# A two-block model on one core: the scratch fill is moved in a queue, columns are waited for by pairs, norms are done by token halves

## The reference, cut to what matters

```python
h = x
for layer in range(2):                       # first block
    if layer == 0:
        h = h + even_mixer(rmsnorm(h))       # short convolution and window means, w_in, w_out
    else:                                    # GLU, 31-tap depthwise convolution, layer norm over channels
        h = h + conformer_conv(rmsnorm(h))
    h = h + cross_attn(rmsnorm(h), mem)      # 4 heads of 256; k, v = split(rmsnorm(mem) @ wkv)
    if layer == 0:
        h = h + swiglu(rmsnorm(h))           # width 2816
    else:
        h = h + moe_swiglu(rmsnorm(h))       # 8 experts of width 3584, the two best per token
x = rmsnorm(h)
h = layer_norm(x)                            # second block
y = hybrid_mixer(h)                          # "fox" attention with forget gates, differential attention, HGRN recurrence
h = layer_norm(ALPHA * h + y)
y = memory_attention(h, mem_2)               # the third attention over a memory
h = layer_norm(ALPHA * h + y)
y = grouped_moe(h)                           # 16 experts of width 512 in 4 groups, two of one group per token
out = layer_norm(ALPHA * h + y)
```

## Time and profile before

| | us |
|---|---|
| median of 3 runs | 2263.54 |
| lowest and highest | 2256.84, 2264.5 |
| profiled execution | 2261.9 |
| its span in the profile | 2260.1 |

### The profile page before, as it was taken

The page is one execution under the profiler, slowest core; times in us unless marked ns, Lnnn a source line. Parts: engine busy times, 40 slices in busy tenths (PEclk is TensorE's granted clock), DMA queues, the critical chain, the costliest instruction groups (busy, mean ns, idle before and its releaser), DMA issues. The chain is left out here.

```text
span 2260.1 us, 30543 instructions
## 1 busy us (share of the span) xinstructions
PE 2184.1 (97%) x11738; PEld 1874.1 (83%) x11738; DVE 1727.9 (76%) x1606; ACT 1362.8 (60%) x1202; POOL 83.3 (4%) x79
## 2 busy tenths in 40 slices
PE   7999999999989999999999999999999999899997
PEld 7888999967877888888888888888779888788886
DVE  4655555697658888888888988888856664698897
ACT  4454433417437777777777777777646344477775
POOL 2000000000001000000000000000000000000000
PEclk9999999999999999999999999999989999999998
DMA  9442565532269999999999999999744161699995
GB/s 303 171 170 93 184 203 190 189 112 75 84 223 354 377 377 381 373 384 376 388 363 392 367 385 368 391 362 396 290 148 160 74 218 44 242 370 380 377 379 214
DMA packets 274825, 617.26 MB, mean 273 GB/s; under 512 B 9537, under 2 KB 34321, under 8 KB 274737
## 3 DMA queue, kind: packets, MB, share of 16 engines
q1 hardware_dynamic: 265648, 584.43, 70.7%
q0 software_dynamic: 9088, 31.60, 4.5%
HBM read 603.41 MB, written 12.58 MB: 273 GB/s over the span
## 5 line engine op out<-in xcount | busy, mean ns | idle before, releaser
L2424 DVE TENSOR_TENSOR w_low<-ring,w_high 128x2048 fp32r<-128x2048 f32 x426 | 971.2, 2290 | 142.3 <-ACT w_high L1705 141.8
L1705 ACT ACTIVATE w_high<-ring 128x2048 fp32r<-128x2048 f32 x426 | 815.1, 1917 | 166.0 <-PE ps L791 166.0
L790 PE MATMUL ps<-w_high,parts 128*128 128x512 f32 (+2 forms) x1896 | 736.5, 388 | 0.0
L789 PE MATMUL ps<-w_high,parts 128*128 128x512 f32 x1560 | 617.9, 396 | 12.6 <-DVE w_low L2424 7.8
L791 PE MATMUL ps<-w_low,parts 128*128 128x512 f32 x1560 | 609.1, 390 | 0.0
L790 PEld LDWEIGHTS ps<-w_high,parts 128*128 128x128 f32 x1896 | 357.6, 189 | 69.3
L789 PEld LDWEIGHTS ps<-w_high,parts 128*128 128x128 f32 x1560 | 293.5, 188 | 74.7 <-DVE w_low L2424 11.6
L1894 DVE TENSOR_TENSOR w_low<-ring,w_high 128x2048 fp32r<-128x2048 f32 (+2 forms) x117 | 262.0, 2253 | 110.3 <-ACT w_high L1428 104.3
L791 PEld LDWEIGHTS ps<-w_low,parts 128*128 128x128 f32 x1560 | 293.1, 188 | 62.7
L789 PE MATMUL ps<-XT_high,w_high 128*128 128x256 f32 x1024 | 294.5, 288 | 9.4 <-DVE parts L1885 7.4
L1428 ACT ACTIVATE w_high<-ring 128x2048 fp32r<-128x2048 f32 (+2 forms) x117 | 219.7, 1884 | 135.4 <-PE ps L791 127.0
(11 more groups left out here) (440 smaller groups left out, 1659.8 us busy)
## 6 DMA issues: line engine op xcount, KB each, us to landing
ring<-in_od_moe_gu SPq DMA_DIRECT2D x224, 1024.0 KB, 8.1
ring<-in_od_moe_down SPq DMA_DIRECT2D x112, 1024.0 KB, 7.8
ring<-in_w SPq DMA_DIRECT2D x96, 1024.0 KB, 8.6
ring<-in_ev_ffn_gu SPq DMA_DIRECT2D x22, 1024.0 KB, 7.6
ring<-in_xa_wkv SPq DMA_DIRECT2D x8, 2048.0 KB, 8.6
ring<-in_od_pw_w SPq DMA_DIRECT2D x6, 2048.0 KB, 8.0
ring<-in_w_in SPq DMA_DIRECT2D x6, 2048.0 KB, 8.0
ring<-in_ev_ffn_down SPq DMA_DIRECT2D x11, 1024.0 KB, 5.1
```

Of the source, the lines that this page charges most:

```text
L789: mm(out_, xh, wh, start=start, stop=False)
L790: mm(out_, xl, wh, start=False, stop=False)
L1705: A(w_high[:, j % SPLITS, :], ring[:, j % NS, :], ACT.Copy).then_inc(moe_sem(k, "high"), 1)
L2424: V.tensor_tensor(w_low[:, j % SPLITS, :], ring[:, j % NS, :], w_high[:, j % SPLITS, :].bitcast(F32), SUB)\
```

## The change

- GpSimd: the two fills of `sums[1]` wait for H and stand ahead of `row(0, ln_in_g_2)`; the fill for k = 2 stays where it was.
- TensorE: `project` of plain units, when first, waits for columns pair by pair. The wait for all columns goes from "B" and from `route(2)`, which now waits pair by pair too.
- TensorE: in "A" the wait for `in_gc` and 20 `keep_busy` transposes ahead of Ak0; `keep_busy` 75 becomes 80 and 90 becomes 50.
- ScalarE: the first six diagonals are written ahead of the copy of Bv1; the first half of fqk is rounded ahead of the squares; a root of a constant loads its table ahead of the norm after the third attention.
- VectorE: the additions Co0 and Co1 are made by halves with accumulated sums, and the norm after them adds those instead of reducing H. Every norm of the second block but the last signals `h_ready` after each half, and fqk and `route(2)` turn H by halves (`turn_by_tokens`).

```diff
...
+            def fill_sums(k, dst):
+                pool.dma_start(sums[k][T:T + P, :], dst[:, 0, :]).then_inc(moe_sem(k, "rows_added"), 16)
+                pool.dma_start(sums[k][0:T, :].rearrange("(a p) d -> p a d", p=P), dst[:, :, :]).then_inc(S("rows_stored"), 16)
+
             def expert_rows(k, source, ready, value, dst):
...
                     pool.wait_ge(S("xs_ready"), 7)
+                    fill_sums(k, dst)
                 else:
-                    pool.wait_ge(S("h_updated"), 4)
-                pool.dma_start(sums[k][T:T + P, :], dst[:, 0, :]).then_inc(moe_sem(k, "rows_added"), 16)
-                pool.dma_start(sums[k][0:T, :].rearrange("(a p) d -> p a d", p=P), dst[:, :, :]).then_inc(S("rows_stored"), 16)
-                if k == 1:
                     pool.wait_ge(S(ready), value)
...
             row(0, ins["od_norm_moe"][0].partition_broadcast(P))
+            pool.wait_ge(S("h_updated"), 4)
+            fill_sums(1, H)
             row(0, ins["ln_in_g_2"].partition_broadcast(P))
...
                 row(0, ins["ln_b_2"][0, j].partition_broadcast(P))
-            expert_rows(2, H, "h_ready", 3, XS)
+            expert_rows(2, H, "h_ready", 6, XS)
...
                         for kc in range(KC):
+                            if first and fb == 0 and kc % 2 == 0:
+                                made = "act" if kc < 4 else "vector"
+                                pe.wait_ge(S("columns_by_" + made), seen[made] - 2 + kc % 4 // 2 + 1)
                             last = mm(pair[:, fb // 2, fb % 2 * T:fb % 2 * T + T], w[:, kc, fb * P:(fb + 1) * P],
...
+            def turn_by_tokens(src, ready, n):
+
+                pe.wait_ge(S("columns_by_act"), seen["act"])
+                pe.wait_ge(S("columns_by_vector"), seen["vector"])
+                seen["act"] += 4
+                seen["vector"] += 4
+                for tc in range(HALVES):
+                    pe.wait_ge(S(ready), n - 1 + tc)
+                    for kc in range(KC):
+                        o = kc % 2 * T + tc * P
+                        last = nc.tensor.transpose(ps[:, 4 + kc // 2, o:o + P], src[:, tc, kc * P:(kc + 1) * P], IDENT)
+                        if tc == 1 and kc % 2:
+                            last.then_inc(S("turned"), 1)
+
             def columns_ready():
...
                 turn(XS, ready, value, parts=(tag != "B"))
-                if tag == "B":
-                    columns_ready()
+                if tag == "A":
+                    evicted("in_gc")
+                    keep_busy(20, 2 * (UNIT["Ak0"] % 2))
                 for name in ("k0", "k1", "v0", "v1"):
...
                 if k == 2:
-                    turn(src, ready, value)
-                    columns_ready()
+                    turn_by_tokens(src, ready, value)
                 pe.wait_ge(S("router_split"), 1)
...
                             turn_half(1)
-                        column_pair(kc)
+                    column_pair(kc)
                     for part in (XT_high, XT_low):
...
                 if k == 1:
-                    keep_busy(75, 0)
+                    keep_busy(80, 0)
                 pe.wait_ge(S("added"), 4 * k)
...
-            turn(H, "h_ready", 1)
+            turn_by_tokens(H, "h_ready", 2)
             upto, ones = c_("upto"), ONES
...
             project("Cv1", halves=(0,))
-            turn_ahead(H, "h_ready", 2)
+            turn_ahead(H, "h_ready", 4)
             project("Cv1", halves=(1,))
...
-            keep_busy(90, 6)
-            route(2, "h_ready", 3, H)
+            keep_busy(50, 6)
+            route(2, "h_ready", 6, H)
             experts(2, H)
...
-            def memory_projections(tag, gain):
+            def memory_projections(tag, gain, diagonal=None):
                 if tag == "B":
...
                         highs(halves_to("pw2_1", -1))
+                        for i in range(DIAGONALS):
+                            diagonal(i)
                     if tag == "C" and j == 1:
...
                     highs(halves_to("value1"))
-            memory_projections("B", ("xa_norm_mem", 8))
-            for b in range(TAPS_ON_PE):
-                for k in range(CONV):
-                    i = b * CONV + k
-                    if i >= DIAGONALS:
-                        act.wait_ge(S("diagonal_used"), i - DIAGONALS + 1)
-                    A(w_(5376, DIAGONALS, P)[:, i % DIAGONALS, :], IDENT, ACT.Copy,
-                      scale=vec("od_dw_w", KC * k + KC - TAPS_ON_PE + b)).then_inc(S("diagonal_ready"), 1)
+            def diagonal(i):
+                b, k = divmod(i, CONV)
+                if i >= DIAGONALS:
+                    act.wait_ge(S("diagonal_used"), i - DIAGONALS + 1)
+                A(w_(5376, DIAGONALS, P)[:, i % DIAGONALS, :], IDENT, ACT.Copy,
+                  scale=vec("od_dw_w", KC * k + KC - TAPS_ON_PE + b)).then_inc(S("diagonal_ready"), 1)
+
+            memory_projections("B", ("xa_norm_mem", 8), diagonal)
+            for i in range(DIAGONALS, TAPS_ON_PE * CONV):
+                diagonal(i)
             act.wait_ge(S("diagonal_used"), TAPS_ON_PE * CONV)
...
             A(table_root, ONES[:, 0:1], ACT.Sqrt)
+            highs(halves_to("fqk", -1))
             squares(H, "moe_done", 1, XS, False)
-            highs(halves_to("fqk", -1))
             layer_norm(w_(6144, HALVES, D))
...
             attention("C", 2, None, None)
+            A(table_root, ONES[:, 0:1], ACT.Sqrt)
             layer_norm()
...
                     ins = V.tensor_tensor(h, h, PAIRS[u % 2], ADD)
+                elif name in ("Co0", "Co1"):
+                    for tc in range(HALVES):
+                        at = 2 * tc + j
+                        ins = V.scalar_tensor_tensor(h[:, tc, :], h[:, tc, :], scale, PAIRS[u % 2][:, tc, :], MUL, ADD,
+                                                     accum_out=halves_sum[:, at:at + 1])
                 else:
...
-            def layer_norm(signal, src=H, beside=None):
+            def layer_norm(signal, src=H, beside=None, summed=False):
                 n_["ln"] += 1
-                step(V.tensor_reduce(mean, src[:, :, :], X, ADD))
+                if summed:
+                    step(V.tensor_tensor(mean, halves_sum[:, 0::2], halves_sum[:, 1::2], ADD))
+                else:
+                    step(V.tensor_reduce(mean, src[:, :, :], X, ADD))
                 V.tensor_scalar(mean, mean, -1.0 / D, None, MUL).then_inc(S("mean_ready"), 1)
...
                     last = V.scalar_tensor_tensor(H[:, tc, :], centred[:, tc, :], rstd[:, tc:tc + 1], b, MUL, ADD)
+                    if tc == 0:
+                        last.then_inc(S(signal), 1)
                 use_row(1 - gain_row[0], last)
+                dve.sem_inc(S(signal), 1)
                 gain_row[0] = 1
-                dve.sem_inc(S(signal), 1)
...
                 last = V.scalar_tensor_tensor(H[:, tc, :], centred[:, tc, :], rstd[:, tc:tc + 1], w_(11264, D), MUL, ADD)
+                if tc == 0:
+                    last.then_inc(S("h_ready"), 1)
             use_row(1, last)
...
             attention("C", 2, None)
-            layer_norm("h_ready")
+            layer_norm("h_ready", summed=True)
...
```

## The result

The changed kernel takes 2245.43 us (median of four runs, 2245.22 to 2245.94); the kernel before 2260.19 (four runs, 2256.47 to 2264.5, three of them those shown above). The ratio is 0.9934, its 95% interval 0.9911 to 0.9957: faster by 0.66%, a little more than the 0.5% that can be told from no change. Forecast were 2247 us. The profiled execution took 2245.53 us, its span is 2243.7.

The account below looks back on a forecast made before the run. TensorE, busy nearly the whole span, was taken as the bound, through its waits and half clock. Terms 9.2 + 2.4 - 0.8 + 0.9 + 5.0 = 16.7 us off 2261.9 gave 2245.2, plus 1.6 for the median: 2247 us, range 2238 to 2255.

Parts of the forecast that it names:

- fills ahead: First mixture: earlier fills on GpSimd end ScalarE's wait and TensorE's wait for piece 3 with its half clock; 9.2 us.
- transposes ahead of Ak0: Ahead of Ak0: 20 transposes fill TensorE's idle time so the matmuls behind run at full clock; 2.4 us.
- columns by pairs, diagonals: Conformer: TensorE's taps end earlier, but VectorE sets the end and half clock follows the idle time; -0.8 us.
- first fqk half: Norm before fqk: rounding moves into ScalarE's idle time, so the centred squares come earlier; 0.9 us.
- norm after the third attention: Sums with the additions, table load ahead, halves and pairs shorten the way to the second router; 5.0 us.
- clock elsewhere: Half clock outside the places the steps name: no term in the forecast sum.
- rival (d): Half clock longer at the conformer, or at Ak0 despite the transposes; costs 2 to 7 us, 2251 us; 16%.
- New half clock outside the conformer: Sign that the forecast is wrong: half clock newly appearing anywhere but the conformer; no size given.
- Rival (a): Fox scores: the half clock at 1675.7 to 1692.7, costing 5 to 7 us, goes away; 2240 us; 15%.
- (b): First mixture: the fill is not what frees ScalarE, or lands late again; only 7.5 us gained, 2256 us; 7%.
- (c): First mixture: the weight stream becomes the bound if a landing takes over about 15 us; 2280 us; 2%.

Follow-up runs that it names:

- 1: The changed kernel with the two fills of sums[1] put back behind row(0, ln_in_g_2) on GpSimd: 2256.0 us.
- 11: The kernel before with only the two fills of sums[1] moved ahead of the row load in GpSimd's queue: 2250.34 us.
- 5: The changed kernel without the 20 transposes ahead of Ak0: 2247.0 us.
- experiment 2: The changed kernel with the full wait for the second memory's columns and all diagonals written after Bv1 is taken, as before: 2244.91 us.
- 8: The changed kernel with the first rounded half of fqk behind the squares again: 2245.78 us.
- experiment 7: The changed kernel with the additions Co0 and Co1 undivided and without sums, the norm reducing H again: 2250.41 us.
- 6: The changed kernel with 90 instead of 50 busy transposes behind the third attention, ahead of the second router: 2249.97 us.
- experiment 9: The changed kernel with ten transposes added in TensorE's 1.24 us idle time ahead of the fox scores: 2238.67 us.
- experiment 3: The changed kernel with 60 instead of 16 busy transposes ahead of the conformer's sums of squares: 2245.49 us.
- experiment 4: The kernel before, unchanged, run and profiled once more: 2258.82 us over ten runs.
- 12: The changed kernel with four idle times filled by transposes, plus transposes ahead of the first router, each scatter and at the last level: 2234.51 us.

## Why the prediction came out

| step | predicted | by the trace | shown by |
|---|---|---|---|
| fills ahead | 9.2 | 9.2 | 1, 11 |
| transposes ahead of Ak0 | 2.4 | 2.5 | 5 (half of it) |
| columns by pairs, diagonals | -0.8 | -0.4 | 2 |
| first fqk half | 0.9 | 1.1 | 8 |
| norm after the third attention | 5.0 | 4.6 | 7 (2.0 of it), 6 (that the 50 are needed) |
| clock elsewhere | 0 | -0.8 | read from the traces |
| not assigned | 0 | 0.1 | |
| sum | 16.7 | 16.3 | |

The sum is that of two profiled executions, 2261.9 and 2245.53 us. By medians the gain is 14.8 us. The forecast put 1.6 us on top of its sum's 2245.2 because the median of three runs lay that much above the profiled one; the changed kernel came out at 2245.43, and the kernel before at 2260.19 instead of 2263.54. That kernel's executions differ by more than this, so the close hit of the median is in part luck.

**Fills.** The step was right: landing before the need, no stall of another kind behind it. Two details of it were not. The prediction timed the larger fill, while ScalarE waits for the smaller; and both landed more slowly than in the kernel before, 8.0 us instead of 5.4 and 11.1 instead of 7.4, where it had taken the 7.4. The slack of 11.8 us covered that.

**Columns and diagonals.** Centring started right behind the third remainder, TensorE stood idle for 5.17 us (5.2 forecast) and the squares' sums took 5.32 (5.3 to 7.4 forecast). The loss came out half as large because L1013 kept to the lower end of its range, and that is this profile's luck: in five other profiles with this edit and the 16 transposes behind the sums (1, 5, 7, 8, 9) L1013 takes 5.54 to 6.45 us, and the stretch from the turning of XS to the next transposes of H, at 572.7 here, is 0.2 to 1.2 us longer. That a part which takes 4.5 us of waits from the busiest engine brings nothing is the part's lesson, and experiment 2 shows it.

**Norm.** By its pieces: up to the mean 4.05 us before, 2.01 now, 2.04 gained where 2.1 was forecast. From there to H 4.12 and 3.16: 0.96, not the table load's 1.28. The mis-sized term is this one: with the load gone the root no longer waits for ScalarE but for VectorE's centring, whose two operations of 1.24 us end at 1925.6; the small step behind them (L1981) releases the root at 1925.87, 0.34 us after ScalarE is through with its squares. I had named no next-latest there. Halves and pairs 1.59, forecast 1.65: the router starts 4.66 us behind the start of H instead of 6.82, and its 16 matmuls spread over 0.57 more. Sum 4.59. Only the 2.04 were undone by themselves (experiment 7); the 0.96 and the 1.59 are read from the two traces. The table load itself takes 1.28 us in both kernels: in the changed one it starts at 1619.93, its activation follows at 1621.23, and taking a load off the path gave 0.96, less than 1.28.

**The clock.** This is where the sum was lucky. New half clock at 18, 1622 and 1947 cost 1.06, 0.73 and 0.93 us, half clock that stayed away at the levels gave 1.96. All is within rival (d), in small pieces of both signs. "New half clock outside the conformer" was one of the prediction's own signs of being wrong, and it is there three times. At the levels the clock fell again in seven of the eight variants 1 to 3 and 5 to 9, all but experiment 2, so the 1.96 are the least certain part of the gain. Rival (a) didn't happen in the changed kernel (0.50 at 1665 to 1680), but its size was about right: experiment 4 shows a run without the fall, 7.8 us shorter there, and experiment 9 takes it away with ten transposes. One program's times vary from run to run, 2254.4 to 2262.97 us in experiment 4. That is not the whole matter here: the changed kernel's four executions lay within 0.7 us with the fall in the profile, and with the 1.24 us of idle time filled all four lay between 2237.96 and 2240.23, 5 to 8 us lower. Rivals (b) and (c) are out: ScalarE's wait is gone, and the stream of weights did not hold up the mixture, 956.4 us, although one landing beside the fills took 18.8 us, more than the 15 that (c) named.

Left open: what decides whether a short idle time is followed by half clock. 5.17 us were in every profile, 1.24 were in ten of eleven profiles and not in experiment 4, and filling one place brought a fall at a later one in experiments 3 and 12 that spent the gain, while in 9 the gain stayed.

## What to carry to other kernels

An engine's wait whose releaser is a DMA issued behind an unrelated wait of another queue was the cheapest thing to remove here (9.2 us in the mixture): look there first, and add up the wait and the half clock behind it. Taking 4.5 us of waits from the busiest engine was worth nothing where VectorE's chain set the end of the stage (experiment 2), so read which engine ends last before and after each edit, and shrink filling work with the wait that it filled. Try filling the idle time just ahead of a long run of small matmuls, which took 6.8 us off the median in experiment 9, and judge such fills by medians over several executions: in experiment 3 half clock was gone at 543 and stood at 661 to 666, and the median was the same.

## What the runs showed of the hardware that I had not expected

The clock stood at half for 17 us (1663 to 1680) while TensorE was busy 5.00 of every 5.00 us, nearly all of it with score matmuls of 64 or 128 rows and 128 or 256 columns; with ten transposes in the 1.24 us ahead of them it stayed at full, and the median was 6.8 us lower. A sum taken with an addition costs little: 0.69 us and a read of 0.08 for 128x512, the next addition starting 0.61 us after the first. A fill of 1 MB took 11.1 us to land beside seven weight pieces and 7.4 where it stood later, and the longest of these pieces took 18.8 us instead of 14.5.
